# A two-layer streaming trunk on one core: forty-four matmuls of constants behind the layer norms' sums left out

## What is computed

```python
z = x @ w_in[l] + b_in[l]
...
merged = sum(sigmoid(gate_k) * (branch_k @ w_branch[l, k]) for k in range(3))
x = layernorm(ALPHA * x + merged @ w_out[l], ln1_g[l], ln1_b[l])
x = layernorm(ALPHA * x + moe(x), ln2_g[l], ln2_b[l])

def layernorm(y, g, b):
    mu = mean(y, -1)
    var = mean(square(y - mu), -1)
    return (y - mu) * rsqrt(var + EPS) * g + b
```

## Time and profile before

| what | value |
|---|---|
| median of 3 executions | 974.74 us (974.45 to 975.25) |
| the profiled execution | 974.62 us |
| its span, first to last instruction | 972.7 us |
| PE busy | 945.3 us (97%) |
| DVE busy | 827.8 us (85%) |
| ACT busy | 693.6 us (71%) |
| POOL busy | 24.9 us (3%) |
| mean granted TensorE clock | 0.997 |

### The profile page before, as it was taken

The page is one execution under the profiler, slowest core; times in us unless marked ns, Lnnn a source line. Parts: engine busy times, 40 slices in busy tenths (PEclk is TensorE's granted clock), DMA queues, the critical chain, the costliest instruction groups (busy, mean ns, idle before and its releaser), DMA issues.

```text
span 972.7 us, 24373 instructions
## 1 busy us (share of the span) xinstructions
PE 945.3 (97%) x9928; PEld 741.5 (76%) x9928; DVE 827.8 (85%) x1495; ACT 693.6 (71%) x1164; POOL 24.9 (3%) x38
## 2 busy tenths in 40 slices
PE   8999999999999999999999999999999999999995
PEld 6877777777776799976578777777777768999663
DVE  6898878776788899999888897778768878999996
ACT  7677665866355899877787666668653669998874
POOL 0000000000002000000110000000000020000002
PEclk9999999999999999999999999999999999999998
DMA  9943644323464399998836355442334434999971
GB/s 358 359 148 118 210 156 135 130 88 130 153 230 139 108 348 386 382 354 329 307 112 232 111 188 157 147 144 90 128 131 157 151 105 157 384 380 380 376 277 56
DMA packets 59941, 205.03 MB, mean 211 GB/s; under 512 B 7248, under 2 KB 10380, under 8 KB 59308
## 3 DMA queue, kind: packets, MB, share of 16 engines
q1 hardware_dynamic: 57036, 198.08, 57.5%
q10 hardware_dynamic: 2784, 5.28, 1.5%
HBM read 198.76 MB, written 3.40 MB: 208 GB/s over the span
## 4 chain that ended last, share of the span: by engine, by line
PE 67%; issue 20%; DVE 6%; ACT 5%; POOL 1%; DVEq 1%; DMA 0%; POOLq 0%; SPq 0%; ACTq 0%
PE bank L2004 39%; PE bank L2028 4%; PE bank L2558 4%; PE bank L2393 3%; DVE wlo L1208 2%; ACT whi L632 2%; PE bank L2033 1%; PE bank L2069 1%; PE bank L2378 1%; POOL acc L616 1%; PE bank L2310 1%; PE bank L2239 1%; PE bank L2077 1%; PE bank L2384 1%; PE bank L2293 1%
## 5 line engine op out<-in xcount | busy, mean ns | idle before, releaser
L1208 DVE SCALAR_TENSOR_TENSOR wlo<-w,whi 128x1024 f16<-128x1024 f32 x356 | 426.4, 1219 | 47.2 <-ACT whi L632 45.6
L632 ACT ACTIVATE whi<-w 128x1024 f16<-128x1024 f32 x356 | 368.6, 1050 | 78.6 <-PE bank L2004 52.0
L2004 PE MATMUL bank<-xhi,whi 128*128 128x320 f16 x680 | 203.7, 300 | 0.0
L2004 PE MATMUL bank<-xhi,wlo 128*128 128x320 f16 x680 | 203.4, 299 | 0.0
L2004 PE MATMUL bank<-xlo,whi 128*128 128x320 f16 x680 | 203.4, 299 | 0.0
L2004 PE MATMUL bank<-arena_b,whi 128*128 128x112 f16 x2048 | 159.6, 213 | 4.6 <-DVE wlo L1208 4.5
L2004 PE MATMUL bank<-arena_b,wlo 128*128 128x112 f16 x1024 | 156.2, 213 | 0.0
L2004 PEld LDWEIGHTS bank<-arena_b,whi 128*128 128x128 f16 x2048 | 149.7, 98 | 7.4 <-issue 4.0
L2004 PEld LDWEIGHTS bank<-arena_b,wlo 128*128 128x128 f16 x1024 | 100.2, 98 | 0.0
L2004 PEld LDWEIGHTS bank<-xhi,whi 128*128 128x128 f16 x680 | 66.5, 98 | 26.6 <-issue 0.4
L2004 PEld LDWEIGHTS bank<-xhi,wlo 128*128 128x128 f16 x680 | 66.5, 98 | 25.9
(11 more groups left out here) (406 smaller groups left out, 1799.4 us busy)
## 6 DMA issues: line engine op xcount, KB each, us to landing
w<-in_w SPq DMA_DIRECT2D x356, 512.0 KB, 5.5
arena_b<-head_rows ACTq DMA_DIRECT2D x2, 1920.0 KB, 9.3
rows<-in_rows SPq DMA_DIRECT2D x2, 1024.0 KB, 9.7
xT<-in_x SPq DMA_DIRECT2D x2, 640.0 KB, 5.4
out_y<-xT SPq DMA_DIRECT2D x4, 320.0 KB
w<-in_w SPq DMA_DIRECT2D x4, 256.0 KB, 5.7
out_ckv<-arena_a SPq DMA_DIRECT2D x2, 320.0 KB
acc<-kr SPq DMA_DIRECT2D x2, 288.0 KB
```

What stands on the lines that cost most here:

```text
L632: A(whi[:, n % SLOTS, :], w32[:, n % RAW, :], ACT.Copy, scale=WS).then_inc(hi_done.sem, 1)
L1208: V.scalar_tensor_tensor(wlo[:, n % SLOTS, :], w32[:, n % RAW, :], WS, whi[:, n % SLOTS, :], ALU.mult, ALU.subtract).then_inc(lo_done.sem, 1)
L2004: ins = M(out, w[:, s, sub * P:(sub + 1) * P], rhs(part, k), start=(n == 0), stop=(n == 3 * len(subs) - 1))
```

## The change

The call of `unread` at the end of `stats` is left out; the function itself stays and is called by nothing.

```diff
                 a.then_inc(ln_ps.sem, 1)
-                if l < L - 1 or k == 0:
-                    unread((4, 2)[k], (14, 16)[k])
```

## The result

The changed kernel takes 979.37 us (median of 6 executions, 976.88 to 980.51), the kernel before 974.84 (6 executions, 974.39 to 975.25). The ratio is 1.0043, with a 95% interval of 1.0033 to 1.0053: 4.5 us slower. The profiled execution is the slowest of the six, so it shows the upper end of what the change costs. It took 980.51 us with a span of 978.4 us, 5.7 us more than the span of before, and its mean granted clock is 0.991 instead of 0.997. In the experiments further down, one execution each of `e_over`, `e_half`, `e_four` and of the kernel before took 1398 to 3444 us, and the ratios leave these four out.

What follows compares the result with a forecast made beforehand. PE was taken as the bound, except in three idle stretches where the norm is. Removed matmuls gain 0; clock falls at three places cost 3 x 1.75 = 5.25 us on 974.62, giving 979.9 us, range 974.2 to 984.0.

Steps and rivals of the forecast that it cites:

- The removed work is worth nothing by itself: At the three norms, the 44 unread matmuls' 6.5 us lie where PE would otherwise wait; removing them gives nothing.
- The norm beside them does not get faster: DVE and ACT take 2.21 us with or without unread matmuls beside them; gain 0, at most 0.4 us.
- The clock falls at 3.6 us of idle: Behind each norm, 3.6 us idle is nearer the 4.8 us that fell than the 1.70 us survived.
- The price of a fall: Behind each norm, about 3.5 us at half speed puts PE 1.75 us behind; bounds 0 and 3.5 us.
- a low clock of 7 us: Sign that the forecast is wrong on the size of the loss: the low clock lasts 7 us.
- Nothing hides it: Behind the norms PE is the bound for over 11 us, so each place costs its 1.75 us in full.
- The clock holds: Rival: the clock does not fall within 3.6 us of idle at the three waits; 974.6 us, chance 0.25.
- a shorter norm: Rival: without PE's writes to banks 4 and 2 the norm gets faster; 974.2 us, chance 0.03 including something not seen.
- Falls at some places only: Rival: the clock falls at one place, 976.4 us, chance 0.10, or at two, 978.1 us, chance 0.12.
- a long climb: Rival: each fall costs up to 3.5 us; two places 981.6 us, three 985.1; chance 0.14.

Runs made afterwards that it cites:

- e_over: Kernel before with forty unread matmuls in each of the three places instead of 14, 16 and 14; ratio 1.0060 to the kernel before.
- e_half: Kernel before with 7, 8 and 7 unread matmuls instead of 14, 16 and 14; median 977.27 us against 974.69, ratio 1.0024.
- e_four: Kernel before with four unread matmuls in a row behind norm 1 in both layers instead of fourteen, sixteen kept behind norm 2; ratio 1.0021.
- e_more: Kernel before with 24 unread matmuls behind norm 1 in both layers instead of fourteen; median 975.20 us against 974.85, ratio 1.0005.
- e_spread: Kernel before with four single unread matmuls spread over norm 1's steps in both layers instead of fourteen in a row; 977.42 us against 974.87, ratio 1.0021.
- e_again: The changed kernel, without the unread matmuls, unaltered and profiled a second time; 978.51 us.
- after: First profile of the changed kernel, all 44 unread matmuls left out against the kernel before; that execution took 980.51 us.
- e_narrow: Kernel before with all unread matmuls kept but 16 columns each instead of 320; median 979.55 us against 974.69, ratio 1.0045.

## Why the prediction was right

*The forecast*, 979.9 us with falls in all three places, met 979.37 us, and the range held it. The mechanism is the one forecast: longer idles, a fall to 1.2 GHz, slow first passes that nothing makes up for. The profiled execution has the three falls, and lost 5.48 us in them where 5.25 were expected. That the number came so near is in part luck: the reason for the falls was wrong, and the median is a mixture of executions, as the points below say.

*The removed work is worth nothing by itself.* Right: the waits for ACT took up all of it, 4.8 to 10.8 us. `e_more` shows that more work in the room behind norm 1 costs nothing either, and `e_over` that it costs once the room is full.

*The norm beside them does not get faster.* Right as far as the waits show: 3.6 us of idle, which is the old 1.70 or 1.43 plus what was removed.

*The clock falls at 3.6 us of idle.* It did in five of the seven places without unread matmuls. But the reason given was wrong. I had compared lengths of single idles, 1.9 us above one bound and 1.2 us below the other, and taken the nearer. `e_spread` falls with idles of at most 0.80 us, `e_half` holds in two places with 2.65 us, and `e_again` holds in two places with 3.6 us. The step that failed is this comparison. In its place the runs put how little TensorE works over the whole norm, and a moment that differs from run to run; what sets that moment stays open. The Trainium skill (TensorE: Matmul & The Clock Gate, "HAM oscillation — how this bites in real kernels") says that idle gaps between bursts bring the clock down. The trace of the changed kernel agrees with its three idles of 3.6 us, but `e_again` held through two such idles, and `e_spread` fell without any above 0.80 us.

*The price of a fall.* The estimate of 1.75 us, from the program's start, is right in kind: low stretches of 3.4 us cost 1.41 and 1.68 us. It is 1.41 where a part of the low stretch lies in the idle, where it costs nothing. It missed the long stretches of 6.8 us, which cost 2.4 to 2.5 us. They came in the three places where the clock fell 1.3 us or more before the first pass (`after`, `e_narrow`, `e_again`); in the nine other falls it fell less than 0.5 us before the first pass or after its start. The prediction named a low clock of 7 us as the sign that its size was wrong. It came in one place of the profile after, and so that place cost more than 1.75 us. The two others cost less, and the sum hides it.

*Nothing hides it.* Right: the place losses and the start add up to the span's growth, 5.74 of 5.7 us, and `e_over` moved the end by its delays.

*The rivals.* "The clock holds" is out for the program as a whole, and "a shorter norm" is out. "Falls at some places only" and "a long climb" are both true of single executions: one place fell in `e_again`, and one of three climbs was long in the first profile. The six executions lie 2.0 to 5.7 us above the kernel before, so the median of 4.5 us is most likely a mixture of these (two executions of the changed kernel were profiled). Three places at 1.75 us is right as a sum and not as a description of every execution.

## What to carry to other kernels

Work whose result nobody reads can still be worth its place, if it keeps TensorE's clock up across a wait: before taking out such matmuls, look at what TensorE does right behind that wait, and whether it is the bound there. Judge the risk by the whole stretch of little work, and not by the longest gap: here four matmuls sprinkled over it didn't help, nor did four in a row, and fourteen in a row did. Look at several profiles, because each shows another set of falls.

## What the runs showed that I had not expected

In all twelve falls that the profiles hold behind these three norms the low clock lasted about 3.4 us (nine times) or about 6.8 us (three times). The clock fell even 0.5 to 0.9 us after the first pass had begun (`e_spread`: pass at 312.23 and 793.12, low in the windows from 312.70 and 794.05). And TensorE needed 1.3 us to go on behind the arm of the mixture, a wait that the profile puts down to ACT and that hides in the norm with sixteen unread matmuls there, but not with 26.
